# Second attention of a two-block transformer kernel: scaling of the probabilities moved from VectorE into TensorE's turns

## The reference

```
def masked_softmax(s, mask):
    p = jax.nn.softmax(jnp.where(mask, s, NEG_INF_2), axis=-1)
    return jnp.where(mask, p, 0.0)

# fox_mixer, 4 heads
        s = jnp.einsum('bqhd,bkhd->bhqk', qi, k).astype(jnp.float32) * scale + (ci[..., :, None] - c[..., None, :])
        p = masked_softmax(s, kpos[None, :] <= t[:, None])
        return jnp.einsum('bhqk,bkhd->bqhd', p.astype(v.dtype), v)

# nsa_mixer, 4 heads, three attentions each (compressed, selected, window)
        p_c = masked_softmax(s_c, dist_c >= 0)
        o_c = jnp.einsum('bhqn,bnd->bqhd', p_c.astype(vc.dtype), vc)
        ...
        return gi[:, :, 0, :, None] * o_c + gi[:, :, 1, :, None] * o_s + gi[:, :, 2, :, None] * o_w
```

## Time and profile before

| | |
|---|---|
| median of 3 executions | 781.91 us |
| profiled execution | 780.94 us |
| its span | 779.1 us |
| TensorE busy | 743.9 us, 95% |
| VectorE busy | 550.8 us, 71% |
| ScalarE busy | 450.3 us, 58% |
| GpSimd busy | 64.8 us, 8% |
| mean granted TensorE clock | 0.99 |

### The profile page before, as it was taken

One profiled execution on the slowest core, in us unless ns is written; L12 is line 12 of the kernel. 1 busy time (PEld: TensorE's weight loads), 2 busy tenths in 40 slices (PEclk: granted clock), 3 DMA queues, 4 the chain that ended last, 5 costly groups with the idle time before them and its releaser, 6 DMA issues.

```text
span 779.1 us, 14673 instructions
## 1 busy us (share of the span) xinstructions
PE 743.9 (95%) x5310; PEld 683.2 (88%) x5310; DVE 550.8 (71%) x1064; ACT 450.3 (58%) x857; POOL 64.8 (8%) x94
## 2 busy tenths in 40 slices
PE   3899999999999999999999999979899999999997
PEld 2799897899999899999999998768798999999997
DVE  4876359898897766666666787567876867677773
ACT  5567466666655655454555766478764655545552
POOL 8001020000545000000000003000000000000000
PEclk9999999999999999999999999999999999999999
DMA  9997897888796566665666576422154765666621
GB/s 293 348 258 239 190 229 221 270 275 272 244 313 201 154 198 183 194 188 169 200 189 163 117 204 162 138 82 95 42 162 140 222 202 165 194 191 180 182 87 55
DMA packets 186933, 148.24 MB, mean 190 GB/s; under 512 B 13662, under 2 KB 171296, under 8 KB 186872
## 3 DMA queue, kind: packets, MB, share of 16 engines
q1 hardware_dynamic: 183008, 143.61, 62.5%
q10 hardware_dynamic: 2232, 3.03, 2.1%
q0 software_dynamic: 1648, 1.00, 0.5%
HBM read 146.29 MB, written 1.36 MB: 190 GB/s over the span
## 4 chain that ended last, share of the span: by engine, by line
PE 86%; ACT 4%; DVE 3%; DMA 3%; issue 1%; POOL 0%; SPq 0%; ACTq 0%; DVEq 0%; POOLq 0%
PE ps L2257 20%; PE ps L1870 15%; PE ps L1871 15%; PE ps L1872 15%; PE ps L2259 10%; DMA raw<-in_w_in 2%; DMA raw<-in_w_ada 1%; ACT w_hi L706 1%; PE ps L2236 1%; DVE w_lo L1203 1%; PE ps L2127 1%; PE ps L2344 1%; PE ps L1918 1%; PE ps L2149 1%; PE ps L2114 1%
## 5 line engine op out<-in xcount | busy, mean ns | idle before, releaser
L1203 DVE TENSOR_TENSOR w_lo<-raw,w_hi 128x1024 fp32r<-128x1024 f32 (+3 forms) x223 | 269.6, 1230 | 73.6 <-ACT w_hi L706 72.2
L706 ACT ACTIVATE w_hi<-raw 128x1024 fp32r<-128x1024 f32 (+3 forms) x223 | 226.2, 1038 | 26.6 <-DMA raw<-in_w_in 7.7
L2257 PE MATMUL ps<-h,w_hi 128*128 128x512 f32 x672 | 239.4, 396 | 0.0
L2259 PE MATMUL ps<-h,w_lo 128*128 128x256 f32 x672 | 189.6, 282 | 0.0
L2257 PEld LDWEIGHTS ps<-h,w_hi 128*128 128x128 f32 x672 | 126.3, 188 | 28.7
L1870 PE MATMUL ps<-h,w_hi 128*128 128x256 f32 (+1 forms) x440 | 127.9, 291 | 6.6 <-DVE h L1276 3.6
L2259 PEld LDWEIGHTS ps<-h,w_lo 128*128 128x128 f32 x672 | 126.2, 188 | 0.0
L1872 PE MATMUL ps<-h,w_lo 128*128 128x256 f32 (+1 forms) x440 | 124.7, 283 | 0.0
L1871 PE MATMUL ps<-h,w_hi 128*128 128x256 f32 (+1 forms) x440 | 124.6, 283 | 0.0
L1870 PE MATMUL ps<-g_hi,w_hi 128*128 128x256 f32 x352 | 98.6, 280 | 0.4 <-DVE g_lo L1535 0.4
L1871 PE MATMUL ps<-g_lo,w_hi 128*128 128x256 f32 x352 | 98.4, 280 | 0.0
(11 more groups left out here) (363 smaller groups left out, 1107.1 us busy)
## 6 DMA issues: line engine op xcount, KB each, us to landing
raw<-in_w_in SPq DMA_DIRECT2D x53, 512.0 KB, 5.7
raw<-in_w_down SPq DMA_DIRECT2D x44, 512.0 KB, 4.2
raw<-in_w_gate_up SPq DMA_DIRECT2D x44, 512.0 KB, 4.1
raw<-in_w_ada SPq DMA_DIRECT2D x32, 512.0 KB, 4.8
raw<-in_w_gate SPq DMA_DIRECT2D x22, 512.0 KB, 4.0
raw<-in_w_up SPq DMA_DIRECT2D x22, 512.0 KB, 5.1
raw<-in_w_ada SPq DMA_DIRECT2D x32, 256.0 KB, 6.7
raw<-in_w_o SPq DMA_DIRECT2D x8, 512.0 KB, 5.0
```

The source lines that it names most:

```text
L706: A(w_hi[:, m % HL, 0:w], raw[:, n % RAW, 0:w], ACT.Copy).then_inc(hi_done, 1)
L1203: V.tensor_tensor(w_lo[:, m % HL, 0:w], raw[:, n % RAW, 0:w], w_hi[:, m % HL, 0:w].bitcast(f32), sub).then_inc(lo_done, 1)
L2257: T.matmul(bank[:, :], hi, h2[:, k, :, :].rearrange("p a b -> p (a b)"), start=(k == 0), stop=False, skip_group_check=True)
L2259: ins = T.matmul(bank[:, 0:SEQ], lo, h_hi[:, k, :], start=False, stop=(k == KC - 1), skip_group_check=True)
```

## The change

VectorE no longer scales `z` in the second block's jobs. It only makes the reciprocal (times mask and gate) and raises `rec_ready`. GpSimd makes from it, for each of the two token tiles, a diagonal matrix: the identity with each row multiplied by that token's reciprocal, 128 x 128 (`diagonal`), and raises `p_ready`. Before it overwrites a diagonal it waits for the turn two jobs back. TensorE's turn multiplies `z` with the diagonal, an f32 matmul with `z` as the stationary and the diagonal as the moving operand, in place of the transpose. The first block's jobs stay as they were. The diagonals lie in the memory of `nrm3` and `tot`. At the first use of `nrm3` a wait on a semaphore of its own becomes a wait on VectorE's own counter.

```
-        nrm3 = sb("nrm3", [P, SEQ])[:, :]
-        tot = sb("tot", [P, SEQ])
+        shared = sb("shared", [P, 2, SEQ])
+        nrm3 = shared[:, 0, :]
+        tot = shared[:, 1, :]
+        diag = shared[:, :, :].rearrange("p g (t b) -> p g t b", t=TT)
...
             def probabilities(g):
                 kind, h = ALL[g]
                 dve.wait_ge(s("e_ready"), 2 * (g + 1))
+                if kind == "F":
+                    line(V.reciprocal(pair(rec, g), pair(den, g)), "rec_ready")
+                    return
                 line(V.reciprocal(pair(rec, g), pair(den, g)))
                 line.settle()
+                if g < N1:
+                    for t, z in enumerate(z_parts(g)):
+                        line(V.tensor_scalar(z, z, pair(rec, g)[:, t:t + 1], None, mult), "p_ready")
+                    return
                 if kind == "C":
...
-                if kind in "SWC":
-
-                    b = 4 * "CSW".index(kind) + h
-                    line(V.tensor_tensor(pair(rec, g), pair(rec, g), gate2[:, :, b:b + 1].rearrange("p t a -> p (t a)"), mult))
-                    line.settle()
-                for t, z in enumerate(z_parts(g)):
-                    line(V.tensor_scalar(z, z, pair(rec, g)[:, t:t + 1], None, mult), "p_ready")
+                b = 4 * "CSW".index(kind) + h
+                line(V.tensor_tensor(pair(rec, g), pair(rec, g), gate2[:, :, b:b + 1].rearrange("p t a -> p (t a)"), mult),
+                     "rec_ready")
...
-                            line(V.tensor_copy(nrm3, NRM3), "nrm3_copied")
-                            dve.wait_ge(s("nrm3_copied"), 1)
+                            line(V.tensor_copy(nrm3, NRM3))
+                            line.settle()
...
+            def diagonal(g):
+
+                pool.wait_ge(s("rec_ready"), g - N1 + 1)
+                if g >= N1 + 2:
+                    pool.wait_ge(s("pt_done"), g - 1)
+                for t in range(TT):
+                    line(G.tensor_scalar(diag[:, g % 2, t, :], ident[:, :], pair(rec, g)[:, t:t + 1], None, mult), "p_ready")
+            for g in range(N1, N1 + N2):
+                diagonal(g)
...
                 if ALL[g][0] == "C":
                     for t in range(TT):
-                        ins = T.transpose(turned(g)[0:NCMP, t * P:(t + 1) * P], zc[:, g % 2, t, 0:NCMP], ident[:, :])
+                        ins = T.matmul(turned(g)[0:NCMP, t * P:(t + 1) * P], zc[:, g % 2, t, 0:NCMP], diag[:, g % 2, t, :],
+                                       start=True, stop=True)
+                elif g >= N1:
+                    for b in range(3):
+                        ins = T.matmul(turned(g)[:, b * P:(b + 1) * P], z_buf(g)[:, b * P:(b + 1) * P],
+                                       diag[:, g % 2, min(b, 1), :], start=True, stop=True)
                 else:
```

## The result

The changed kernel took 790.12 us (median of 4 runs, 788.69 to 795.29) against 780.86 us for the kernel before (4 runs): ratio 1.0115, 95% interval 1.0071 to 1.0159. A second set of runs gave 792.17 against 781.38 us, ratio 1.0124 (1.0091 to 1.0156). It is slower, as forecast, but by 9 to 11 us where 3.5 us were forecast, outside the range of 782.1 to 787.7 us. The profiled execution took 788.69 us, with a span of 786.9 us against 779.1 us. Three executions of the later experiments, one of e9 and two of e11, took 1207 to 4158 us and are left out of every figure.

What follows compares the result with a forecast made beforehand. TensorE bounds pairs 0 to 4, the ScalarE-VectorE chain pairs 5 to 7. Products 3.1, first handover 0.1, pairs 5 and 6 0, pair 7 0.22 + 0.1: +3.5 us, 784.4 us profiled, 785.4 median; range 782.1 to 787.7.

Steps and rivals of the forecast that it cites:

- the products: TensorE's turns: each transpose replaced by a product costs 0.111 us more, 3.1 us in pairs 0 to 4, 0.22 in pair 7.
- rival 4: TensorE's turns: a product costs hardly more than a transpose, 783.2 us, within 0.3% of no change; chance 0.12.
- rival 5: VectorE's scalings: faster, because its 0.55 us per job is what counted; chance 0.06, together with gains not seen.
- Rival 3: Pair 0's turn: products raise TensorE's clock up to 1.1 us sooner, saving 0.5 us, 784.9 us; chance 0.08.
- I take 0.3 us, nearer to the copy: GpSimd's price for one 128x128 diagonal, between 0.2 us from the copy and 0.46 us from two-input operations.
- Behind turn a, six slow records cover job b's diagonals: Pair 0: the second job's diagonals are hidden behind the first job's turn; first handover +0.1 us (-0.1 to +0.45).
- Handing over costs nothing there: Pair 7: diagonals ready at 554.2 us against 554.29 for scaled halves; 0.1 us added for disturbance, range 0 to 1.4.
- rival 1: Pairs 6 and 7: GpSimd's diagonals come late, held up by VectorE's operations, 786.2 to 786.8 us; chance 0.14.
- rival 2: Half-clock stretch moves from pair 6 to the output projection, half of its 3.3 us added, 787.1 us; chance 0.10.
- get smaller in sum: TensorE's gaps in pairs 5 to 7 shrink in total, given as argument against a half-clock stretch landing on bound work.

Runs made afterwards that it cites:

- e9: Kernel before, with TensorE's waits in second attention filled by products of the identity with itself; 782.01 us, ratio 0.9982.
- e11: Changed kernel, with pair 0's reciprocals ahead of VectorE's weight split and TensorE's waits filled by identity products; 786.55 us, ratio 1.0048 to the kernel before.
- e1: Kernel before, with second attention's turns multiplying VectorE's scaled probabilities by the identity (f32 product) instead of transposing, GpSimd idle; 786.82 us, ratio 1.0070.
- e3: Changed kernel, with the diagonals made by VectorE instead of GpSimd; 785.00 us, ratio 1.0052 to the kernel before.
- e8: Changed kernel, with TensorE's longer waits in second attention filled by products of the identity with itself; 788.46 us, ratio 1.0079 to the kernel before.
- e10: Kernel before, with pair 0's probabilities ahead of VectorE's weight split and TensorE's shorter waits filled by identity products; 778.76 us, ratio 0.9957.
- e2: Kernel before, scaling and transposes kept, but GpSimd also makes the diagonals, unread, and each turn waits for them; 786.50 us, ratio 1.0073.

## Why the prediction was wrong

**Right: the products.** Six products more cost 0.67 us a pair on TensorE (e1: 2.7 us over pairs 0 to 3), the four of pair 4 0.64 us where 0.44 us was forecast, and the 0.66 us of pair 5 vanished in the wait for ScalarE, 0.96 to 0.23 us, where about 0.3 us was forecast. A factor of 2 between product and transpose held; rival 4, a cheap product, and rival 5, VectorE's time as what counts, fell. Rival 3 is not borne out: with products in pair 0's turn (e1) the granted clock was 0.70, 0.50 and 0.94 in the stretches of 2 us from 512 us on, with transposes 0.70, 0.50 and 0.95 in those from 510 us on, so half clock lasted 3.4 us either way.

**The step that failed: "I take 0.3 us, nearer to the copy".** A diagonal of 128x128 took 0.585 to 0.60 us, outside my own bounds of 0.2 to 0.46 us. The error was to scale the copy's 0.61 us with its columns: the earlier trace rows would have allowed that nearly all of it is fixed, and 0.61 us belonged in the range. With 0.6 us, a job's diagonals are ready 1.3 us behind the reciprocal, not 0.7. The step "Behind turn a, six slow records cover job b's diagonals" fell too: turn a waited for GpSimd, and GpSimd began job b's diagonals only then; the second of them met VectorE's split and took 1.40 us. Pair 0's gathering came 3.14 us later, of which 0.76 us was there before the stage: 2.4 us in place of the 0.76 us forecast for it (0.1 for handing over and 0.66 for six products). Pairs 1 to 4 then added 2.7 us where 2.4 us was forecast.

**Pairs 6 and 7: "Handing over costs nothing there".** From pair 5's gathering to pair 7's last turn the offset grew from 5.87 to 7.56 us, 1.7 us in place of the 0.1 us forecast for it. VectorE's chain ran 5.86 us later at pair 6 and at pair 7 alike, so pair 6's own lateness (0.7 us) was covered and the 1.7 us are pair 7's handover. That is rival 1, which I priced at 0.8 to 1.4 us above the forecast and gave a chance of 0.14. The contention I had feared is there (two diagonals took 0.74 us more than alone), and the rest goes with the diagonals' own 0.6 us.

**The clock: rival 2.** I argued that TensorE's gaps in pairs 5 to 7 "get smaller in sum" and so gave it 0.10. They did in the first profile (2.9 us against 3.1 us) and in e1 (3.0 us), and grew to 5.1 us in the changed kernel's second profile. So their sum is not what decides: e1 and e3 show that with products alone the slow stretch can move from pair 6's chunk, paid by the wait behind it, to the output projection, for 1.6 us. In the changed kernel's first profile it did not move, in its second it did, twice as long. Over all runs of the second set the changed kernel had 5.7 us more at half clock than the kernel before, 0.40 x 5.7 = 2.3 us of a mean difference of 9.9 us (791.3 against 781.4 us). e8, e9 and e10, without slow stretches in the stage once the waits are filled, show that the waits have a part in bringing them about; e11 shows that filling most of them is not enough.

**The sum.** With means and that slope, at equal half-clock time: products alone (e1) 4.7 us, handover alone (e2) 3.3 us, together 8.0 us; the changed kernel 7.7 us. Each of these is known to about 2 us only, so that the parts add up is consistent with the account and no proof of it. Adding the clock's 2.3 us gives the 10 us. What was forecast at 3.5 us was about the products' own part. Two things stay open: which part of the 4.7 us is the moved slow stretch in an average run, since only one trace shows each experiment, and why the first slow stretch falls at 485 us in some executions and at 497 us in others, ahead of all changed code. It makes 1.7 us of difference at 492 us between profiles and is part of the spread of 7 us among the kernel before's runs.

## What to carry to other kernels

An operation handed to another engine is not priced by scaling a larger tile's row: if that is the one row at hand, its full duration belongs in the range, and where the next engine already waits, each such operation is counted in full. A gap ahead of TensorE can cost twice, once as a wait and once as the half clock behind it, so look where that slow stretch lands: ahead of another wait it was free here (e9), on bound work it cost about half its length (e1). Changing the order on the engine that is waited for, with the gap filled, gave here what a lighter engine did not.

## What the runs showed of the hardware

- GpSimd: an f32 tensor-by-scalar operation of 128x128 took 0.60 us, a copy of 128x512 0.61 us, a two-input operation of 128x256 with both inputs broadcast 0.62 us. Across these forms the size hardly shows, but a two-input operation of 128x32 took 0.25 us, and no form ran in two sizes apart from that one, so how much of the 0.60 us is fixed stays open.
- The same diagonal took 1.40 us beside a VectorE split of 128x1024 (1.21 us).
- TensorE's clock went to 1.2 GHz also in a stretch in which TensorE was busy throughout (484 to 490 us, granted clock 0.72 in the changed kernel's profile, 1.00 in the kernel before's, with the same instructions).
- Slow stretches came in two lengths in the changed kernel's two profiles, with the same instructions: 3.4 us and 6.8 us from pair 0's turn on (granted clock 0.79 and 0.57 in 512 to 520 us).
- Useless products ahead of the waits halved the changed kernel's time at half clock (21.3 to 10.8 us), with 3.5 us less time by the ratios, at the edge of the intervals. In the kernel before 7.2 us less at half clock went with 1.2 us less time.
